# Two blocks of a causal convolution as dense products over groups of 64 channels, and a new order in the first ten attention steps

## The reference

```
u = proj[..., o3:]
c = u[..., :512] * sigmoid(u[..., 512:])
c = causal_dwconv(c, cv_dw_w) + cv_dw_b      # y[t] = sum over k of w[k] * c[t - 30 + k], k = 0..30
c = silu(layernorm(c, cv_ln_g, cv_ln_b))
y = concatenate([a, c]) @ w_out              # a: the attention half
```

## Time and profile before

| what | value |
|---|---|
| median of 3 runs | 1279.99 us (1279.79 to 1280.47) |
| the profiled execution | 1277.17 us, span 1275.4 us |
| TensorE busy, and its granted clock | 1239.7 us (97%), mean 0.996 |
| VectorE, ScalarE, GpSimd busy | 776.0, 590.5, 753.3 us |
| read from HBM | 130.88 MB |

### The profile page before, as it was taken

How to read it: one execution, slowest core, us unless ns; L and a number is a source line. 1 busy time by engine, 2 the same in 40 slices (tenths; PEclk the granted TensorE clock), 3 DMA queues, 4 the chain that set the end, 5 groups by cost and what they waited for, 6 DMA issues and landing times.

```text
span 1275.4 us, 16982 instructions
## 1 busy us (share of the span) xinstructions
PE 1239.7 (97%) x6162; PEld 1032.8 (81%) x6162; DVE 776.0 (61%) x1271; ACT 590.5 (46%) x964; POOL 753.3 (59%) x864
## 2 busy tenths in 40 slices
PE   5999999999999999999999999999999999999997
PEld 4777878878888888887778988887888888888887
DVE  5868788436554466798877436764367516641654
ACT  3375667457774446233456654444334323331341
POOL 2634444434344676686446977436559958875782
PEclk9999999999999999999999999999999999999998
DMA  9422224232345633232224443212313332333322
GB/s 379 180 67 76 85 83 140 97 100 87 121 132 191 215 111 99 83 101 86 85 69 163 138 146 116 83 50 82 93 58 108 116 108 84 98 100 99 99 83 67
DMA packets 43108, 142.73 MB, mean 112 GB/s; under 512 B 4881, under 2 KB 7441, under 8 KB 41873
## 3 DMA queue, kind: packets, MB, share of 16 engines
q1 hardware_dynamic: 42768, 141.39, 34.1%
q10 hardware_dynamic: 256, 0.26, 0.1%
HBM read 130.88 MB, written 8.39 MB: 109 GB/s over the span
## 4 chain that ended last, share of the span: by engine, by line
PE 70%; DVE 20%; ACT 6%; issue 3%; POOL 1%; DMA 1%; DVEq 0%; SPq 0%; ACTq 0%; POOLq 0%
PE ps L126 69%; DVE tm L139 5%; ACT tm L133 3%; DVE tm L136 3%; DVE ma L139 1%; DVE ac L139 1%; ACT L133 1%; PE ps L130 1%; DVE spl L136 1%; DVE sph L147 1%; DVE tm L144 1%; DVE x L139 1%; DVE ewl L136 1%; DVE zh L147 1%; DMA x<-xin 1%
## 5 line engine op out<-in xcount | busy, mean ns | idle before, releaser
L136 POOL TENSOR_TENSOR wl<-raw,wh 128x256 fp32r<-128x256 f32 x804 | 695.8, 897 | 463.8 <-ACT wh L133 456.2
L133 ACT ACTIVATE wh<-raw 128x1024 fp32r<-128x1024 f32 x201 | 212.1, 1056 | 307.2 <-PE ps L126 301.3
L126 PE MATMUL ps<-hh,wh 128*128 128x512 f32 x872 | 344.2, 395 | 0.0
L126 PE MATMUL ps<-hh,wl 128*128 128x512 f32 x872 | 340.4, 390 | 0.0
L126 PE MATMUL ps<-hl,wh 128*128 128x512 f32 x872 | 340.4, 390 | 0.0
L126 PEld LDWEIGHTS ps<-hh,wl 128*128 128x128 f32 x872 | 164.1, 188 | 34.8
L126 PEld LDWEIGHTS ps<-hh,wh 128*128 128x128 f32 x872 | 164.2, 188 | 33.3 <-DVE tm L139 0.4
L126 PEld LDWEIGHTS ps<-hl,wh 128*128 128x128 f32 x872 | 164.3, 188 | 33.0
L139 DVE SCALAR_TENSOR_TENSOR tm<-cb,par_sb,tm 128x512 f32<-128x512 f32 x88 | 87.1, 990 | 50.5 <-ACT tm L133 47.1
L136 DVE TENSOR_TENSOR tm<-tm,tm 128x512 f32<-128x512 f32 (+4 forms) x113 | 93.3, 830 | 40.1 <-ACT tm L133 37.3
L133 ACT ACTIVATE tm<-tm 128x512 f32<-128x512 f32 (+3 forms) x109 | 54.1, 531 | 80.4 <-DVE tm L139 64.3
(11 more groups left out here) (308 smaller groups left out, 2254.0 us busy)
## 6 DMA issues: line engine op xcount, KB each, us to landing
raw<-units SPq DMA_DIRECT2D x201, 512.0 KB, 3.5
ada<-units SPq DMA_DIRECT2D x16, 512.0 KB, 14.7
kept<-ge SPq DMA_DIRECT2D x16, 256.0 KB, 3.0
tm<-kept SPq DMA_DIRECT2D x16, 256.0 KB, 3.7
tm<-gate_w SPq DMA_DIRECT2D x12, 256.0 KB, 4.2
x<-xin SPq DMA_DIRECT2D x2, 1024.0 KB, 6.3
x<-xin SPq DMA_DIRECT2D x1, 2048.0 KB, 11.2
out<-x SPq DMA_DIRECT2D x16, 128.0 KB, 1.8
```

The source lines that it names most:

```text
L126: return self.none if self.e is None else self.e.matmul(out, lhs, rhs, start=start, stop=stop, skip_group_check=skip)
L133: return self.none if self.e is None else self.e.activation(out, in_, func, **kw)
L136: return self.none if self.e is None else self.e.tensor_tensor(out, a, b, op)
```

## The change

The diagonal products become dense ones. A block of 128 channels is taken as two groups of 64. `MVh[g]` and `MVl[g]` hold 64 channels twice: on the group's own 64 partitions, and on the other 64 shifted by two columns. A weight matrix of 128x128 then covers, for each of the 64 channels, two input shifts and two output shifts, so that one matrix does the work of four taps; eight matrices (one unit) make a group. The bank's own half and its other half, one column later, are added to give the result. So there are four units for blocks 2 and 3 in place of eight, and 4 x 8 x 3 = 96 products in place of 2 x 31 x 3 = 186. Blocks 0 and 1 stay with VectorE. Around it: ScalarE writes the high parts into both places (`rows_high`) and copies the low part across (`rows_low_copy`), VectorE subtracts (`rows_low_half`); ScalarE copies the bank's other half to `LAP`, and VectorE adds the halves and the bias (`conv_join`). The first four halves stay ahead of step 0; the other four go to steps 0, 2, 4 and 6.

```
-CW_HALVES = (2, 2, 1, 1, 1, 1, 1, 1, 1, 0, 1, 0, 0, 0, 0, 0)
+CW_HALVES = (1, 0, 1, 0, 1, 0, 1, 0, 0, 0, 0, 0, 0, 0, 0, 0)
+DENSE = (2, 3)
+CW_UNITS = [("cw", j, g) for j in DENSE for g in range(2)]
...
# TensorE
-        def cw(j, q, part):
+        def conv(x):
+            name, part = CW_UNITS[x // 2], x % 2
...
             if part == 0:
+                take(1)
+                pe.wait_ge(s_pad, 1)
+                pe.wait_ge(s_mvl, j, g)
+                pe.wait_ge(s_mvs, j, g)
+                pe.wait_ge(s_wh, name)
+            for n in range(4 * part, 4 * part + 4):
+                w, t = slice(128 * n, 128 * n + 128), slice(4 * n, 4 * n + T)
+                pe.mm(PS[1][:, :], WH[s][:, w], MVh[g][:, t], n == 0, False)
+                pe.mm(PS[1][:, :], WH[s][:, w], MVl[g][:, t], False, False)
+                pe.wait_ge(s_wl, name)
+                last = pe.mm(PS[1][:, :], WL[s][:, w], MVh[g][:, t], False, n == 7)
+            if part:
+                last.then_inc(*s_unit.up(name))
+                bank[1] = (s_ac, (j, g))
...
+            if n < KV_STEP:
+                dproj(h, step)
+                if n and n % 2 == 0:
+                    pv_d(n // 2 - 1)
+                if n in (5, 9):
+                    sub_sum(n // 4 - 1)
+                if n == 7:
+                    sub_out(0)
+                filler(n)
+                if step == 4:
+                    dproj(h, 5)
+                qk_d(n + 2)
...
             turn_d(n)
...
# ScalarE
+        def rows_high(k):
...
+            act.fn(MVh[g][own, 30:30 + T], HOLD[j][own, :], ACT.Copy).then_inc(*s_mvh.up(j, g))
+            act.fn(MVh[g][other, 28:28 + T], HOLD[j][own, :], ACT.Copy)
+
+        def rows_low_copy(k):
...
+            act.wait_ge(s_mvl, j, g)
+            act.fn(MVl[g][other, 28:28 + T], MVl[g][own, 30:30 + T], ACT.Copy).then_inc(*s_mvs.up(j, g))
...
         def conv_out(x):
...
+                act.fn(LAP[own, 1:T], PS[1][other, 0:T - 1], ACT.Copy).then_inc(*s_lap.up(j, g))
...
         for n in range(16):
...
+            if n < KV_STEP:
+                join_d(n + 1)
+                dproj(h, step)
             if n and n % 2 == 0:
                 pv_d(n // 2 - 1)
...
+            for x in convs:
+                conv_out(x)
+            if n < KV_STEP:
+                turn_d(n)
             if n < 14:
                 qk_d(n + 2)
...
# VectorE
+        def rows_low_half(k):
...
+            dve.wait_ge(s_mvh, j, g)
+            dve.tt(MVl[g][own, 30:30 + T], HOLD[j][own, :], f32(MVh[g][own, 30:30 + T]),
+                   ALU.subtract).then_inc(*s_mvl.up(j, g))
+
+        def conv_join(x):
...
+            dve.wait_ge(s_lap, j, g)
+            dve.stt(AC[j][own, :], PS[1][own, :], par_sb[own, POFF["cv_dw_b_2"] + j:POFF["cv_dw_b_2"] + j + 1],
+                    LAP[own, :], ALU.add, ALU.add).then_inc(*s_ac.up(j, g))
...
-            taps((0, 6, 6, 14)[j])
+            taps((0, 6, 6, 7)[j])
+            if j == 3:
+                rows_low_half(0)
+                rows_low_half(1)
+                taps(7)
...
         dproj(0, 1)
-        taps(3)
+        taps(5)
         dproj(0, 2)
+        conv_join(1)
+        conv_next(1)
         taps(3)
         dproj(0, 4)
         taps(3)
         dproj(0, 5)
+        conv_join(3)
+        conv_next(3)
         taps(3)
...
             h, step = d_step(n)
-            if step is not None:
+            if n < KV_STEP:
+                join_d(n + 1)
                 dproj(h, step)
...
             if step == 4:
                 dproj(h, 5)
+            if n < KV_STEP:
+                qk_d(n + 2)
             turn_d(n)
+            for x in range(cw_done(n), cw_done(n + 1)):
+                conv_join(x)
             if step == 1:
                 dproj(h, 2)
...
# the weights, on the host
+            j, g, c = u[1], u[2], np.arange(64)
+            for q, r, m in itertools.product(range(8), range(2), range(2)):
+                x = 4 * q + 2 * (r != g) - (m != g)
+                if 0 <= x < 31:
+                    b[64 * r + c, 128 * q + 64 * m + c] = w["cv_dw_w_2"][0][x, 128 * j + 64 * g + c]
```

More of the change, by code:

```diff
@@ L213, in unit_order @@
         step = D_STEP.get(n, (0, 0))
-        more = [("cw", 2 + x // 8, x // 2 % 4) for x in range(done, done + CW_HALVES[n]) if x % 2]
+        more = [CW_UNITS[x // 2] for x in range(done, done + CW_HALVES[n]) if x % 2]
         done += CW_HALVES[n]
@@ L341, in build @@
     cp0 = off[0]
[L342 to L349, removed]
+    PADDED = T + 32
+    CPF = at("cpf", [P, 2, PADDED], F32)
+    o_ac = (off[0], off[0] + 2048, cp0, off[0] + 4096)
+    off[0] += 2 * 2048
+    mv0 = off[0]
+    MVh = [at(f"mvh{i}", [P, PADDED], F32R) for i in range(2)]
+    MVl = [at(f"mvl{i}", [P, PADDED], F32R) for i in range(2)]
+    o_yc = [cp0 + 4 * PADDED] + [mv0 + 4 * PADDED * j for j in range(1, 4)]
+    off[0] = cp0 + 17152
     AC = [at(f"ac{j}", [P, T], F32, o_ac[j]) for j in range(4)]
-    LM = at("lm", [P, 384], F32, cp0 + 6912)
+    HOLD = [at(f"hold{j}", [P, T], F32, sq0 + 2048 * (j - 1)) if j in DENSE else None for j in range(4)]
+    LAP = at("lap", [P, T], F32, sq0 + 6144)
+    LM = at("lm", [P, 384], F32, cp0 + 4352)
     v20 = off[0]
@@ L934, in dproj @@
             bank[b] = (s_rx, (nm, h, 2))
-        def cw(j, q, part):
-            s = PLACE["cw", j, q] % RING
+        def conv(x):
+            name, part = CW_UNITS[x // 2], x % 2
+            j, g = name[1:]
+            s = PLACE[name] % RING
             if part == 0:
[L940 to L954, removed]
+                take(1)
[12 more added lines that the diff above has]
+                bank[1] = (s_ac, (j, g))
         def qk_d(n):
@@ L1086, in tensor_program @@
                     pv_d(n // 2 - 1)
-                if n <= KV_STEP:
+                if n == KV_STEP:
                     qk_d(n + 2)
-                if step is not None:
-                    dproj(h, step)
                 if n > KV_STEP:
@@ L1093, in tensor_program @@
             else:
-                if step is not None:
-                    dproj(h, step)
                 if n < 14:
                     qk_d(n + 2)
-                if n in (5, 9, 13):
-                    sub_sum(n // 4 - 1)
-                if n in (7, 11, 15):
+                if n == 13:
+                    sub_sum(2)
+                if n in (11, 15):
                     sub_out(n // 4 - 1)
                 filler(n)
-            if step == 4:
-                dproj(h, 5)
             turn_d(n)
@@ L2766, in pool_program @@
         pool.zero(CPF[:, :, 0:30]).then_inc(*s_pad.up(0))
-        pool.zero(f32(CPAh[:, :, 0:30])).then_inc(*s_pad.up(1))
-        pool.zero(f32(CPAl[:, :, 0:30])).then_inc(*s_pad.up(2))
+        for t in (*MVh, *MVl):
+            last = pool.zero(f32(t[:, 0:30]))
+        last.then_inc(*s_pad.up(1))
+        pool.zero(LAP[:, 0:1]).then_inc(*s_pad.up(2))
         pool.zero(RS[:, :]).then_inc(*s_pad.up(3))
```

118 lines of the change are left out of this document (67 added, 51 removed).

## The result

The change makes the kernel slower: 1285.03 us median (1281.92 to 1290.16, 12 runs) against 1279.89 for the kernel before in the same session (12 runs), ratio 1.0041 with a 95% interval of 1.0029 to 1.0053. The prediction was 1279.0, with 1285.0 as the upper end of its range. A later session with the experiments gave 1284.14 and a ratio of 1.0038 [1.0027, 1.0049], so the loss is real.

What follows compares the result with a forecast made beforehand. It took an attention chain on VectorE and ScalarE to bound steps 0 to 9. Steps -5.2, start of step 0 +2.8 and `join_d(10)` +1.4 gave -1.0 us: 1279.0 from 1279.99, range 1271.0 to 1285.0.

Steps and rivals of the forecast that it cites:

- Start of step 0: Ahead of step 0: VectorE's added work makes the rotation wait, so step 0 starts 2.8 us late (bounds 0 and 5.3).
- A: Steps 0 to 9: the forecast itself, the attention chain on VectorE and ScalarE binds before and after, 1279.0 us; chance 0.50.
- C: Steps 1, 5, 9: TensorE's clock falls in its new gaps, three falls cost 5.1, so +4.1, 1284.1 us; chance 0.22.
- the 21 us that go: Steps: 90 convolution products fewer at 0.233 us each, 21.0 us of TensorE, claimed not to be on the path.
- B: Steps 0 to 9: TensorE was the pace, so waits of 8.3 us don't come back; -9.3, 1270.7 us; chance 0.27.
- D: Convolution: the products are no fewer than before, though the code counts 96; chance 0.01.
- VectorE's work: Steps 0 to 9: VectorE's busy time falls from 61.3 to 59.0 us, by taps, joins and less contention; -2.3.
- VectorE's waits: Steps 0 to 9: VectorE's waits fall from 14.0 to 11.1 us, 2.9 less; joins stay at 2.8.
- `ath`: Steps 0 to 9: VectorE's 8.7 us of waits for `ath` go; 4.2 return in steps 3 and 7, 0.8 in 2 and 6.
- the rotation: Steps 1, 5, 9: VectorE's wait for the rotated result lies open, 0.7 x 3 = 2.1 us (bounds 0 and 2.0 each).
- `rth`, `rx` and the rotation DMAs: Steps 0 to 9: VectorE's waits for these behind a join, 0.3 to 0.5 us each, 1.2 together.
- Wrong altogether: Behind 740 us: a stage there getting longer or shorter would show the forecast wrong, since nothing there is touched.

Runs made afterwards that it cites:

- e1: The changed kernel plus 60 stand-in products on constants, at five places where TensorE waited: 1280.29 us, ratio 1.0008.
- e6: The changed kernel plus 8 stand-in products on constants, ahead of `pv_d(4)` only: 1281.89 us, ratio 1.0026.
- e15: The changed kernel itself, unedited, measured again in the session of the experiments: 1284.14 us, ratio 1.0038.
- e9: The kernel before with one edit, its last half unit of convolution (9 products) issued in step 9 instead of step 10: 1281.56 us, ratio 1.0015.
- e3: The kernel before, diagonal convolution kept, in the change's new order of steps, last half unit at step 9 instead of 10: 1283.28 us, ratio 1.0035.
- e7: e3 plus 8 stand-in products on constants ahead of `pv_d(4)`: 1279.41 us, ratio 1.0003 to the kernel before.
- e2: The kernel before with 92 of its 186 convolution products left out, order and units unchanged, output incomplete: 1280.3 us, ratio 1.0009.
- e4: The change's dense products (two blocks) in the old order of steps: 1280.31 us, ratio 1.0010 to the kernel before.
- e13: Three dense blocks in the old order, plus 12 stand-in products on constants ahead of each of `pv_d(3)` and `pv_d(4)`: 1274.58 us, ratio 0.9965.
- e5: e4 plus 64 stand-in products on constants, ahead of rotations in steps 1, 5, 9 and of `pv_d(1)`, `pv_d(3)`, `pv_d(4)`: 1288.70 us, ratio 1.0081.
- e10: The changed kernel with its last half unit of dense products (12 products) at step 10, ahead of `pv_d(4)`, instead of step 6: 1283.72 us, ratio 1.0026.
- e12: e4 with its last half unit of dense products at step 10, ahead of `pv_d(4)`, instead of step 6: 1288.63 us, ratio 1.0066.
- e14: e4 plus 12 stand-in products on constants ahead of `pv_d(4)`, in the finished convolution's bank: 1279.21 us, ratio 0.9997.

## Why the prediction was wrong

**The two paths, split.** From the first convolution product to `ydh` the change's trace takes 6.94 us longer than that of before (175.73 against 168.79). Start of step 0: `join_d(0)` comes 33.38 us after the first landmark, 31.79 before: +1.6. Steps up to `pv_d(4)`: 78.99 against 76.82, +2.2; in e1, at full clock, 76.50, so -0.3 is the chain and +2.5 the clock. Behind `pv_d(4)`: 63.36 against 60.18, +3.2, all of it clock by e6: the half clock that begins at 679.5 lasts until 693, 6.7 us beyond `pv_d(4)`, of which half is lost. Chain +1.3, clock +5.7. This is the split of two single traces, and it is more than the 5.1 of the medians: the trace of before is one of that kernel's best executions. The second trace of the change (e15) takes 4.5 us more than that of before, with only two falls of 3.4 us from 679 on, and 1.6 of them behind `pv_d(4)`. That the clock takes most of the loss holds in both, and e1 says so without the traces (ratio 1.0008); the exact shares do not.

**The step that failed is the choice between A and C.** The text priced C at +4.1 us and gave it 0.22, because "off those points the steps hide it". The mechanism that it named is the one that the runs show, and it even named `pv_d(4)` and the first `kv` as the points that decide. The forecast's own sum, -1.0, has no term for the clock at all; the runs put some 4 of the 5.1 us there (the change against e1 by the ratios: 4.2 us, and 3.8 with e15). That C's 1284.1 stands so near the 1285.0 measured is in part luck, since it adds too low a chain to falls that came at other places. What the text didn't do is read the points that it named. The sum said of the 21 us that go "their cover is what is left of the chain" and stopped there: it never asked what each removed product had been covering. In the trace of before the nine products of `conv(15)` stand in the one gap that is followed by 58 us of products that hardly wait. Issuing them a step earlier costs 1.7 us (e9), of which a part is the later rotation; in the new order, where they are gone from this place too, eight stand-ins there give back the whole loss (e3, e7). And C was priced with three falls of the rotations in steps 1, 5 and 9, alike; the falls came in steps 1, 3 and 5, and a long one from the rotation of step 9 into `kv`. What lies ahead of `pv_d(4)`, three falls and half of the fourth, 20 us at half clock, cost 2.5 us; the 6.7 us behind it cost 3.2.

**B** (TensorE was the pace) is refuted by e2: 21 us less for TensorE, no gain, and 12 us of idle in its steps. **D** is refuted by the 96 product rows.

**The terms of the sum**, without the clock (e1):
- Start of step 0: +2.8 forecast, +1.6 measured. The rotation did wait, but 1.24 us and not 2.8. (By its own rows the text should have had 3.2: `rtl` at 585.1 and the 1.6 us from there to the rotation make 586.7, not 586.3.) The two `rows_low_half` ahead of the first landmark took 1.22 and 1.12 us, as priced; the two between the projections, priced at 1.18 too, took 0.67 and 0.68. `conv_join` was right (0.69 forecast, 0.73 to 0.76 measured). The contention that the Trainium skill describes (GPSIMD Engine Reference, section 1, Specifications) shows here again: most taps take 1.10 to 1.22 us where GpSimd works beside them and 0.75 where it is idle. But GpSimd worked beside all four `rows_low_half`; beside the two short ones its own subtraction was the one that took longer, 1.29 and 1.26 us where most take 1.19. Which of the two engines is held up, the rows of before could not tell.
- VectorE's work from `join_d(0)` to `pv_d(4)`: 61.1 before, 60.0 in e1, so -1.1; forecast -2.3 and +1.4 for `join_d(10)`, together -0.9. Right.
- VectorE's waits, -2.9 forecast: 14.2 before and 14.7 in e1, +0.5. `ath` was forecast at 5.0 and took 3.6, the rotation 2.1 and 2.5, the joins 2.8 and 3.8. The term that missed is the last, "`rth`, `rx` and the rotation DMAs ... 1.2": the DMAs alone took 3.2 in steps 3 and 7, the maxima waited 1.2 for TensorE.

So the chain would have come out at +1.3 instead of -1.0: no change, the forecast's own case, had the clock stayed.

**What would show it**, point by point: 96 products, yes. Rotation "near 586": 585.9 in e1 with a first landmark 1.3 late, so 584.6 beside the trace of before. `ath` waits of about 2 us in two steps: 1.6 and 1.1. Some 20 idle us of TensorE: 17.7 of 79. `pv_d(4)` within 2 us of 678: 3.8 late by landmarks. C's mark, "a clock under 1.00 between 602 and 690": yes. "Wrong altogether" did not happen: behind 740 nothing changed.

The Trainium skill spoke for C (TensorE: Matmul & The Clock Gate, Part 1): idleness takes the full clock back. The traces agree (0.87 in the thinned steps, 1.00 with e1's stand-ins), and with it the case was to be decided by reading which gaps a critical product ends.

**What stays open.** Why e9 falls for 3.4 us and e3 for 6.8 after nearly the same wait (3.31 and 3.18), and why e3's fall costs four us and e4's, as long and at the same place, less than two. Why both traces of the change have a long fall ahead of the first landmark (last section), and whether a part of its 5.1 us lies there. Whether the 2 us by which `pv_d(4)` is later in e7's trace than in that of before exist in the medians, which show no difference: the profiled run of before is one of its best.

## What to carry to other kernels

Before products are taken from TensorE, list the gaps that they stand in, and price each by what ends it: a gap that ends in a product somebody waits for, or in a long stretch of products with no waits, can cost the clock as well as itself. If such a gap can't be filled with work, a few products of constants fill it at no cost that these runs show (e7, e13), provided that their PSUM bank is free when they are issued (it was not in e5). Real work as the cover has one condition more: in e10 to e12 its result had to be read before the next products could write the same bank, and those waited 4.8 to 6.2 us. Stand-ins in that very bank, which nobody has to read, made no such wait (e13, e14). And read an experiment that frees an engine only together with the clock: three dense blocks looked worthless (1279.6) until 24 idle products made them worth nearly 5 us.

## What was not expected of the hardware

A fall can come where TensorE is busy nearly all the time by the profile (4.75 of 5 us, then 9 of 9). In the change's trace the clock is 0.86 from 495 to 500 and 0.51 from 500 to 509, in a stage that is the same in both kernels, and the first landmark is 4.4 us late:

```profile
495.00:500.00 5.00, 4.75 (x26) 4.08 (x26) 2.49 (x3) 2.50 (x4) 3.78 (x4) 0.86 0.50 117
500.00:509.00 9.00, 9.00 (x30) 7.73 (x30) 1.08 (x7) 1.65 (x3) 2.62 (x4) 0.51 0.14 53
```

Ahead of it stand 16 products of a single column each:

```profile
495.28 2.19 PE L127 MATMUL ps<-con_raw,tm 128*128 128x1 f32 x16 [0.17 <-DVE tm L137]
```

The same 16 stand in the trace of before, where the clock stayed at 1.00, so this fall comes in some executions and not in others; eight of the seventeen traces of this study have one there. Nine have none, and their first landmark lies at 569.0 to 569.7; six have 3.4 us of half clock, and it lies at 570.5 to 572.4; the two of the change have 10.2 us, and it lies at 573.8 and 573.9. That explains most of why single spans of these kernels differ by 3 us and more, and why stages have to be compared between landmarks. That the one-column products bring it about is not shown. Nor is it the change's code: e1, e6 and e10 run the same program up to there and have the short fall or none. Also new was how cheap the remedy is: 8 products, 1.9 us of array time, against 3.4 to 4.1 us of the kernel's.
